# A two-block model on one core: one softplus for both first gates, the forget gate's softplus under a key projection, an attention gate projection moved up, weights split ahead of a norm

## The reference

```python
# first block, each of 2 layers: h = rmsnorm(x), proj = h @ w_in, then three branches
beta = sigmoid(gb); g = -exp(a_log) * softplus(ga + dt_bias)      # delta rule's gates
o_a  = rmsnorm(gated_delta_rule(q, k, v, g, beta)) * silu(gz)
o_b  = causal_block_attention(...) * silu(mz)                     # 8 heads, gate mz of width 1024
log_a = -8 * r * softplus(-a_param)                               # linear recurrence (LRU)
o_c  = scan(exp(log_a), sqrt(1 - exp(2 * log_a)) * (i * u)) * silu(lz)
x = x + concat(o_a, o_b, o_c) @ w_out

# second block, each of 2 layers
x = x + 0.5 * swiglu(rms_norm(x), w_gate, w_up, w_down)           # FFN, inner width 2816
mem_n = rms_norm(mem)                                             # 256 memory tokens
x = x + mixer(rms_norm(x), mem_n) @ w_out
x = x + 0.5 * swiglu(rms_norm(x), ...)
# after the first of them: keys, values and forget gates for the second layer's attention
kvf = rms_norm(x, kv_norm) @ w_kv
log_f = log_sigmoid(kvf[..., 1536:] + fox_f_bias)                 # 12 heads, by a softplus
```

## Time and profile before

| | us |
|---|---|
| median of 3 runs | 1812.42 (1811.76 to 1814.68) |
| profiled execution, its time | 1812.14 |
| its span (first to last instruction) | 1810.4 |
| PE busy (11578 matmuls) | 1674.7, 93% |
| PE weight loads busy | 1539.8, 85% |
| DVE busy (1542 instructions) | 1055.8, 58% |
| ACT busy (1295) | 872.3, 48% |
| POOL busy (72) | 97.9, 5% |
| mean granted clock of PE | 0.968 of 2.4 GHz |

### The profile page before, as it was taken

One profiled execution on the slowest core, in us unless ns is written; L12 is line 12 of the kernel. 1 busy time (PEld: TensorE's weight loads), 2 busy tenths in 40 slices (PEclk: granted clock), 3 DMA queues, 4 the chain that ended last, 5 costly groups with the idle time before them and its releaser, 6 DMA issues.

```text
span 1810.4 us, 27224 instructions
## 1 busy us (share of the span) xinstructions
PE 1674.7 (93%) x11578; PEld 1539.8 (85%) x11578; DVE 1055.8 (58%) x1542; ACT 872.3 (48%) x1295; POOL 97.9 (5%) x72
## 2 busy tenths in 40 slices
PE   6999899999989899899888999998998899789999
PEld 6989687989968798889887899987997798679998
DVE  6875564886555555445786645454544456555544
ACT  4975364586445534335545533343452447443332
POOL 0012000012200000000240000000000001000000
PEclk9999999999999899999999999998999999989999
DMA  6624034553304465445422555543564454025553
GB/s 204 196 66 141 35 95 139 151 154 90 107 31 134 160 209 185 140 163 164 134 75 70 163 187 186 187 126 119 191 195 148 155 165 155 30 87 186 185 184 103
DMA packets 204296, 253.22 MB, mean 140 GB/s; under 512 B 17808, under 2 KB 183952, under 8 KB 204048
## 3 DMA queue, kind: packets, MB, share of 16 engines
q1 hardware_dynamic: 204176, 251.49, 43.7%
HBM read 250.43 MB, written 1.05 MB: 139 GB/s over the span
## 4 chain that ended last, share of the span: by engine, by line
PE 79%; DVE 9%; issue 5%; ACT 4%; POOL 1%; DMA 1%; SPq 0%; DVEq 0%; ACTq 0%; POOLq 0%
PE bank L784 78%; ACT arena L1357 3%; DVE weights_rest L1861 2%; PE bank L825 1%; DVE arena L2007 1%; DMA ring<-in_w_in 1%; ACT L1352 0%; DVE small L2177 0%; DVE small L1889 0%; DVE arena_parts L1949 0%; DVE x L2223 0%; DVE weights_rest_more L1861 0%; ACT weights_high L1357 0%; DVE xT_rest L1949 0%; POOL arena L2491 0%
## 5 line engine op out<-in xcount | busy, mean ns | idle before, releaser
L784 PE MATMUL bank<-xT_high,weights_high 128*128 128x256 f32 (+1 forms) x2352 | 683.5, 291 | 41.6 <-DVE weights_rest L1861 32.0
L784 PE MATMUL bank<-xT_rest,weights_high 128*128 128x256 f32 (+1 forms) x2352 | 673.2, 286 | 0.0
L784 PE MATMUL bank<-xT_high,weights_rest 128*128 128x256 f32 (+1 forms) x2048 | 585.8, 286 | 0.0
L1861 DVE TENSOR_TENSOR weights_rest<-ring,weights_high 128x1024 fp32r<-128x1024 f32 (+3 forms) x414 | 486.1, 1225 | 96.7 <-ACT weights_high L1357 93.3
L1357 ACT ACTIVATE weights_high<-ring 128x1024 fp32r<-128x1024 f32 (+3 forms) x414 | 399.6, 1019 | 236.4 <-PE bank L784 224.4
L784 PEld LDWEIGHTS bank<-xT_high,weights_high 128*128 128x128 f32 (+1 forms) x2352 | 457.6, 195 | 55.6 <-DVE weights_rest L1861 35.5
L784 PEld LDWEIGHTS bank<-xT_rest,weights_high 128*128 128x128 f32 (+1 forms) x2352 | 458.0, 195 | 3.1 <-issue 2.0
L784 PEld LDWEIGHTS bank<-xT_high,weights_rest 128*128 128x128 f32 (+1 forms) x2048 | 398.4, 195 | 0.5
L1357 ACT ACTIVATE arena<-bank 128x512 f32<-128x512 f32 (+4 forms) x249 | 134.4, 553 | 426.5 <-PE bank L784 361.9
L784 PE MATMUL bank<-arena 128*128 128x128 f32 (+2 forms) x1416 | 206.5, 304 | 42.1 <-ACT arena L1357 26.9
L784 PEld LDWEIGHTS bank<-arena 128*128 128x128 f32 (+1 forms) x1416 | 177.7, 201 | 69.4 <-ACT arena L1357 25.9
(11 more groups left out here) (179 smaller groups left out, 1712.1 us busy)
## 6 DMA issues: line engine op xcount, KB each, us to landing
ring<-in_w_in SPq DMA_DIRECT2D x36, 1024.0 KB, 5.2
ring<-in_ffn_w_gate SPq DMA_DIRECT2D x36, 1024.0 KB, 5.4
ring<-in_ffn_w_up SPq DMA_DIRECT2D x35, 1024.0 KB, 5.4
ring<-in_ffn_w_down SPq DMA_DIRECT2D x34, 1024.0 KB, 4.9
ring<-in_w_out SPq DMA_DIRECT2D x22, 1024.0 KB, 4.9
ring<-in_w_in_a SPq DMA_DIRECT2D x11, 1024.0 KB, 5.3
ring_more<-in_ffn_w_down SPq DMA_DIRECT2D x10, 1024.0 KB, 4.9
ring_more<-in_ffn_w_up SPq DMA_DIRECT2D x9, 1024.0 KB, 5.3
```

What stands on the lines that cost most here:

```text
L784: return eng.matmul(o, a, b, start=first, stop=last)
L1861: TTs(rest_slot(b)[:, part], raw_slot(b)[:, part], high_slot(key)[:, part].bitcast(F32), ALU.subtract).then_inc(*dv.mark(("rest", key, z)))
```

## The change

Four things change, and nothing of the computation.

- `spl` is gone. `abt` puts the four negated `a_param` columns beside the eight of the delta rule's gate, and one softplus of twelve columns serves both. The result is read from the shared tile; the LRU's part is multiplied by -8 into `csp`.
- A stage `fox_s` between `f 0` and `k 2` holds ACT's exponential and all of DVE's part of the former `fox_d`. ACT's three constant copies and PE's product stay in `fox_d`.
- `mz 1` stands between `sm 0` and `gdn_o 1`; `mz 2` and `mz 3` come in the iterations of hp = 1 and 2, and none in that of hp = 3. The first four steps of `outp` are cut in two by the `parts` of head pair 2.
- At the start of each `norm_part` ACT and DVE split two more blocks, the next pair's gate and up blocks, before they wait for PE's transposes. Formerly these were split in the `ffn` stage behind it.

```diff
--- before.py
+++ after.py
@@ -173,12 +173,12 @@
             for n in range(2):
                 out += [("tri", l, n, s)] + beside[s][n] + [("trid", l, n, s)]
         m = f"m{l}"
-        out += [("gdn_o", l, 0), ("att", m, 0), ("sm", m, 0), ("gdn_o", l, 1)]
+        out += [("gdn_o", l, 0), ("att", m, 0), ("sm", m, 0), proj("mz", 1), ("gdn_o", l, 1)]
         o = ("outp", f"h{l}", 16)
         ready = {1: ["c", "a"], 2: [("b", 0)], 3: [("b", 1)]}
         for hp in range(1, 4):
-            out += [("att", m, hp), ("pv", m, hp - 1), ("sm", m, hp), ("parts", f"h{l}", *ready[hp]), ("proj", l, "mz", hp)]
-        out += [("parts", f"h{l}", ("b", 2)), (*o, 0, 4), ("pv", m, 3), ("parts", f"h{l}", ("b", 3)), (*o, 4, 16)]
+            out += [("att", m, hp), ("pv", m, hp - 1), ("sm", m, hp), ("parts", f"h{l}", *ready[hp])] + ([proj("mz", hp + 1)] if hp < 3 else [])
+        out += [(*o, 0, 2), ("parts", f"h{l}", ("b", 2)), (*o, 2, 4), ("pv", m, 3), ("parts", f"h{l}", ("b", 3)), (*o, 4, 16)]
     out.append(("final",))
     for l in range(2):
 
@@ -214,7 +214,7 @@
             out += [("pv", "x", 5), ("parts", "s1", ("x", 4), ("x", 5)), (*o, 6, 8)]
         out += [("norm", f"f2{l}", "x", f"ffn2_norm{l}"), ("ffn", f"f2{l}", 0, PAIRS)]
         if l == 0:
-            out += [("norm", "kv", "x", "kv_norm"), ("pk", "k", 0), ("pk", "k", 1), ("pk", "f", 0), ("pk", "k", 2), ("fox_d",)]
+            out += [("norm", "kv", "x", "kv_norm"), ("pk", "k", 0), ("pk", "k", 1), ("pk", "f", 0), ("fox_s",), ("pk", "k", 2), ("fox_d",)]
             out += [("pk", "v", 0), ("fox_e",), ("fox_k",), ("pk", "v", 1)]
             out += [("norm_turn", "f11", "x", "ffn1_norm1"), ("pk", "v", 2)]
     return out
@@ -696,7 +696,7 @@
         def small_lnq():
             return small[:, 511:512]
 
-        spn = {("spa", 0): 8, ("spa", 1): 8, ("spl", 0): 4, ("spl", 1): 4, ("spf", 0): 24}
+        spn = {("spa", 0): 12, ("spa", 1): 12, ("spf", 0): 24}
 
 
         @block.sync
@@ -1434,6 +1434,8 @@
                     eng.wait_ge(sems("vec_in"), 16)
                 if id == "n0":
                     split_until(1)
+                if st[0] == "norm_part":
+                    split_until(splits[0] + 2)
                 for k in slices_of(st):
                     if k in (2, 3):
                         continue
@@ -1489,7 +1491,6 @@
                 A(nal, V(f"a_log{l}"), ACT.Exp).then_inc(*ac.mark(("nal", l)))
                 ac.wait_ge(*ac.last())
                 softplus_exp(("spa", l))
-                softplus_exp(("spl", l))
 
             def st_proj(st):
                 _, l, name, j = st
@@ -1813,8 +1814,10 @@
                         ac.wait_ge(*at((f"{z}f", p - 2)))
                     rsqrt(rn2[:, p % 2], ps(g, 2, S), 64, True, frees=g, key=(f"f{z}rn", p), bias=small_ln8() if z == "q" else None)
 
+            def st_fox_s(st):
+                softplus_exp(("spf", 0))
+
             def st_fox_d(st):
-                softplus_exp(("spf", 0))
                 A(minus_row, C("minus_row"), ACT.Copy).then_inc(*ac.mark())
                 A(ident_parts, ident, ACT.Copy).then_inc(*ac.mark())
                 A(diag_parts, C("causal")[:, P:S], ACT.Copy).then_inc(*ac.mark(("mask_parts",)))
@@ -1833,7 +1836,7 @@
                      memkn=st_memkn, memq=st_memq, pa=st_px, pb=st_px, pk=st_px,
                      memke=st_memke, hg_q=st_hg_q, hg_kd=st_hg_kd, hg_g=st_hg_g, hg_d=None,
                      hg_f=st_hg_f, hg_state=st_hg_state, hg_level=None, hg_o=st_hg_o, fox_q=st_fox_norm,
-                     fox_k=st_fox_norm, fox_d=st_fox_d, fox_e=st_fox_e)
+                     fox_k=st_fox_norm, fox_s=st_fox_s, fox_d=st_fox_d, fox_e=st_fox_e)
             for st in sched:
                 ac.stage(st[0], st)
                 if X[st[0]]:
@@ -1933,6 +1936,8 @@
                 id = st[1]
                 if id == "n0":
                     split_until(1)
+                if st[0] == "norm_part":
+                    split_until((pieces[0] + 1) // 2 + 2)
                 high, low = parts_of(st)
                 for k in slices_of(st):
                     g = ("nt", id, k // 2)
@@ -1972,8 +1977,9 @@
                 z = zf[:, :, 0:4]
                 TTs(z, v[:, :, 4:8], over(V(f"dt_bias{l}"), 2), ALU.add).then_inc(*dv.mark(frees=st))
                 dv.wait_ge(*dv.last())
-                zz = sp[:, 4, 16:24]
-                eng.tensor_copy(zz.rearrange("p (a b) -> p a b", a=2), z).then_inc(*dv.mark())
+                zz = sp[:, 4, 12:24]
+                eng.tensor_copy(zz[:, 0:8].rearrange("p (a b) -> p a b", a=2), z).then_inc(*dv.mark())
+                TS(zz[:, 8:12], V(f"a_param{l}"), -1.0, None, ALU.mult).then_inc(*dv.mark())
                 dv.wait_ge(*dv.last())
                 softplus_front(("spa", l), zz)
                 dv.wait_ge(*at(("eb", l)))
@@ -1982,17 +1988,12 @@
                 dv.wait_ge(*dv.last())
                 eng.reciprocal(beta, beta).then_inc(*dv.mark())
                 dv.wait_ge(*dv.last())
-                softplus_back(("spa", l), zz, gg.rearrange("p a b -> p (a b)"))
+                both = sp[:, 3, 0:12]
+                softplus_back(("spa", l), zz, both)
                 for t in range(2):
-                    STT(out=gg[:, t, :], in0=gg[:, t, :], scalar=-1.0, in1=nal, op0=ALU.mult, op1=ALU.mult).then_inc(*dv.mark(("gbeta", l)))
-                    dv.wait_ge(*dv.last())
-
-                zl = sp[:, 4, 8:12]
-                TS(zl, V(f"a_param{l}"), -1.0, None, ALU.mult).then_inc(*dv.mark())
+                    STT(out=gg[:, t, :], in0=both[:, 4 * t:4 * t + 4], scalar=-1.0, in1=nal, op0=ALU.mult, op1=ALU.mult).then_inc(*dv.mark(("gbeta", l)))
+                TS(csp, both[:, 8:12], -8.0, None, ALU.mult).then_inc(*dv.mark(("csp", l)))
                 dv.wait_ge(*dv.last())
-                softplus_front(("spl", l), zl)
-                softplus_back(("spl", l), zl, csp, sign=-8.0)
-                new.at[("csp", l)] = dv.last()
 
             def conv(l, i):
                 taps = V(f"gdn_conv{l}")[:, 4 * i:4 * i + 4] if i < 12 else V(f"lru_conv{l}")[:, 4 * (i - 12):4 * (i - 12) + 4]
@@ -2309,7 +2310,7 @@
                     dv.wait_ge(*dv.last())
                     softplus_front(("spf", 0), zz)
 
-            def st_fox_d(st):
+            def st_fox_s(st):
                 zz = zf.rearrange("p a b -> p (a b)")
                 softplus_back(("spf", 0), zz, zz, sign=-1.0)
                 TS(D_parts, C("restart"), 0.0, None, ALU.mult).then_inc(*dv.mark(("D_zero",)))
```

More of the change, by code:

```diff
@@ L1333, in _ @@
                        hg_f=None, hg_state=st_hg_state, hg_level=st_hg_level, hg_o=st_hg_o, fox_q=st_fox_norm,
-                       fox_k=st_fox_norm, fox_d=st_fox_d, fox_e=None)
+                       fox_k=st_fox_norm, fox_s=None, fox_d=st_fox_d, fox_e=None)
             for st in sched:
@@ L2410, in _ @@
                      hg_f=st_hg_f, hg_state=None, hg_level=st_hg_level, hg_o=None, fox_q=st_fox_norm,
-                     fox_k=st_fox_norm, fox_d=st_fox_d, fox_e=st_fox_e)
+                     fox_k=st_fox_norm, fox_s=st_fox_s, fox_d=None, fox_e=st_fox_e)
             for st in sched:
```

## The result

The changed kernel takes 1757.13 us (median of 4 runs, 1751.86 to 1758.79), the one before on the same chip 1813.1 (1811.76 to 1814.68, 4 runs): a ratio of 0.9686, 95% interval 0.9664 to 0.9708. It is 56.0 us faster; 57.4 was forecast. A second set on another chip gives 1753.37 against 1814.05, ratio 0.9674 (0.9658 to 0.9690). The profiled execution was the fastest of the first four, 1751.86 around a span of 1750.1, 60.3 us under the span before. In it PE is busy 18.3 us less and idle 42.0 less (1810.4 - 1674.7 = 135.7 before, 1750.1 - 1656.4 = 93.7 now).

The account below looks back on a forecast made before the run. TensorE, 79% of the chain that ended last, bounds the kernel, so only its waits and low-clock time can be had. Gains 31.1 + 10.1 + 8.4 + 7.8 = 57.4 from 1812.1 give 1754.7 us; range 1750 to 1771.

Parts of the forecast that it names:

- Part 1: Splitting ahead at `norm_part`: eight FFN waits go, 25.1 us, and slow stretches behind them, 6.0; 31.1 us taken.
- pieces of 17.25 for a pair (none): FFN pairs: a piece of 17.25 us was taken to hold no slow stretch, longer pieces the excess; stretches summed to 6.0.
- Part 2: One softplus of twelve columns at each layer's start: 10.1 us, bounds 5.9 to 11.3.
- some 0.6 stays in the ACT and DVE chain: Each layer's start: ACT's `gq0` copy 1.4 us late, 0.78 idle at 58.69; 0.6 lost, met by PE at 127.80.
- The step on the clock: `gq0` at each layer's start runs at full clock, 5.75 us: 1.5 back in the first layer, 2.7 in the second.
- Part 3: `mz1` before the delta rule's second half: 4.7 us a layer, less 0.5 at `open_acc`; sum 8.4, bounds 2.0 to 9.4.
- the clock would hold in the shorter wait: Wait for `wT`, 2.4 us: clock assumed to hold; if it fell, 5.5 us behind it become 8.3, 2.8 less gain.
- Part 4: Forget gate's softplus beside `k2`: wait of 5.1 us and 2.7 of slow stretch go; 7.8 us, bounds 5.1 to 7.8.
- clock not given back: Rival, whole kernel: stretches at 1.2 GHz come all the same, gain 38.1, time 1774 us; chance 0.14.
- The early gain is returned: Rival, each layer's start: ACT and DVE chain does not move with PE; softplus gain 0 to 2, time 1764; chance 0.12.
- Part 1 does not do what it says: Rival, `norm_part`: DVE finds ACT's high halves not made and the wait stays; time 1786 us; chance 0.03.
- ACT late in part 3: Rival, delta rule: ACT's high halves, table switch before `wT` and waits eat the fill; gain 0 to 2, time 1762; chance 0.14.

Follow-up runs that it names:

- 33.5 alone: Kernel before with only ACT and DVE splitting two blocks more at each `norm_part`: 1780.13 us, ratio 0.9809.
- the two halved versions: Changed kernel with only DVE splitting two blocks ahead at `norm_part`: 1782.79 us; with only ACT doing so: 1795.94 us.
- 7.8 alone: Kernel before with only the single softplus of twelve columns: 1805.84 us, ratio 0.9955.
- 5.6 alone: Kernel before with only `mz 1` moved before `gdn_o 1`, later `mz` and `outp` steps adapted: 1808.09 us, ratio 0.9966.
- 4.7 alone: Kernel before with only the forget gate's softplus moved between `f 0` and `k 2`: 1808.97 us, ratio 0.9973.

## Why the prediction was right, and where its sizes were off

The time, 1754.7, lies 2.4 us under the median of the first chip and 1.3 over that of the second, and the mechanism of each part is in the trace and holds alone. Three terms were mis-sized. That the total came so close is partly luck: in place the four parts gained 60.9 us, 3.5 more than forecast, and the median of the first chip lies 5.3 us above the profiled run in which they were read.

**Part 1** (forecast 31.1; 34.8 in place, 33.5 alone). The waits went whole and the stretches with them. The step that failed is "pieces of 17.25 for a pair (none)": I took 17.25 as an undisturbed pair. It is 16.97; the 17.25 held 0.28 us that PE lost behind the wait even at full clock. The eight pieces shrank by 9.4 us where I had 6.0. Of the 3.3 between, 2.2 are this loss, once for each of eight waits. The other 1.1 is slow clock in the two pieces of three pairs, whose floor I had put at 3 x 17.25 = 51.75, so at 0.91 each: behind a wait but at full clock such a piece takes 51.17, and 52.66 held 1.49. The order in time was as worked out: at the second place DVE's four halves ended at 716.1, ahead of the norm's operations. That the blocks must be split ahead on ACT as well as on DVE in the three other parts of a layer is shown by the two halved versions.

**Part 2** (10.1, upper bound 11.3; 12.0 in place, 7.8 alone). The step "some 0.6 stays in the ACT and DVE chain" failed. ACT took the copy of `gq 0` at 41.83, behind the high halves, but by 52.98 it was 5.71 us earlier than before (58.69 to 52.98): its idle time of 0.78 there took up most of the lag, and PE's wait for POOL stayed at 1.39, not the 2.0 that I had named. That is 1.2 of the 1.9 us. The step on the clock was right: `gq 0` takes 5.75 now. In the second layer 0.9 us came beside the sum, between the norm's transposes and `gq 0`: from them to `lru` 30.1 us instead of 36.7, where the wait and the slow `gq 0` make 5.7 of the 6.6. What the step missed is that the gain does not reach the end in full: in the part alone 2.7 us came back elsewhere, half of it as slow stretches behind the waits of the first FFN.

**Part 3** (8.4; 6.5 in place, 5.6 alone). The wait of 2.4 us and its releaser came as worked out, `mz 1` and all. The Trainium skill (page "ScalarE: Activation LUTs", section "What ACT_TABLE_LOAD costs") has a drain of about 1380 ns beside the load, and an estimate with it would put the wait at 3.8 us. This trace does not agree: the load starts at 208.58, right behind the high halves, and the next ACTIVATE at 209.87, 1.29 later, so no drain stands there. `open_acc` cost nothing in the first layer and 0.85 in the second; I had 0.5. The step that failed is that the clock would hold in the shorter wait: it did in the first layer, fell in the second (2.5 us), and in another profile the first had over 17 us at 0.50 to 0.59. It was priced as a bound, not as a chance. Over the six profiles with this wait the clock held in 2 of 12 places, so the first layer of the profiled run was the lucky case: at 2.0 a layer this part would give 4.

**Part 4** (7.8; 7.6 in place, 4.7 alone). `fDr` starts without a wait and takes 1.06. DVE's chain began at 1190.48, right behind ACT's exponential. In place it was right to 0.2; alone it gave back about 3 us, as Part 2 did, most of it in the second FFN's pieces behind unchanged waits. In the profile of the whole change nearly nothing is returned (60.9 in place, 60.3 at the end), but that is the fastest run, at a mean clock of 0.979; the other three, at 0.975, took 4.8 to 6.9 us more. No profile shows where those lost it; the only profile of such a long run, 1759.21 in the second set, has the long fall behind `wT`.

The rival "clock not given back" (1774) is refuted as a whole, PE's busy time fell by 18.3 us; but its root, that the same wait may or may not bring a slow stretch, is the largest thing left open in the time. "The early gain is returned" and "Part 1 does not do what it says" are refuted by the rows at 122.12 and by the pairs. "ACT late in part 3" (0 to 2 us for the part) is refuted by 6.5 in place and 5.6 alone; the wait was the one foreseen, and what shrank the second layer's gain to 2.0 was the clock.

## What to carry to other kernels

When a stream of PE work waits for a product of two in-order engines, let both run ahead of the stage that they share with it; one alone saved here none or two of eight waits. When a stage is moved earlier on PE, its side work on the other engines need not move with it: put it behind what PE wants next, on each engine of the chain. And measure what an undisturbed stretch takes before using a disturbed one as the floor.

## What the runs showed of the hardware

- The time follows the mean granted clock from run to run: 20 runs of the kernel before lie from 1811.49 us at 0.968 to 1817.69 at 0.963; a straight line through all 20 gives about 1.25 us for each 0.001.
- The same wait does not always bring the same clock: behind 2.41 to 2.43 us in front of `wS` there was no fall in 2 of 12 places; in eight others it lasted for some 3 to 7 us, and in two for over 17. Behind 0.69 us there, `o` ran at full clock in 6 of 6. What decides was not found; no experiment here separates it.
- Behind a wait PE's stream of 128x256 matmuls lost 0.26 to 0.28 us even at the full clock (17.25 against 16.97 for a pair, 51.17 against 50.91 for three).
- A polynomial step of DVE over twelve columns takes 0.2 us (1.62 for a run of eight such steps), as over eight columns (1.59).
